# Six places in two hand-written side-work lists: the context's squares and tables, the mixer's mask and turns

## The reference

```python
for l in range(DEPTH):                       # first block, DEPTH = 2
    h  = rmsnorm(x,  norm_g[l]) * (1.0 + scale[:, None]) + shift[:, None]
    hc = rmsnorm(xc, norm_g[l]) * (1.0 + scale_c) + shift_c
    if last:                                 # second layer: context only gives keys and values
        pkv = hc @ w_in[l][:, OFF_K:OFF_POOL]
    q, k, v, up, uf, g = split_proj(h @ w_in[l])
    q = apply_axial_rope(rmsnorm(q, q_norm_g[l]), cos, sin)
    k = apply_axial_rope(rmsnorm(k, k_norm_g[l]), cos, sin)
    ...
# second block ("mixer"): gated spatial part and linear recurrence
h = _rmsnorm(x, norm1_g);  p = h @ w_in      # p = [u, v, g_lru, x_lru]
v = _layernorm(gelu(v)); w = where(tril, ws, 0)
y_gm = gelu(u) * (einsum('hts,bcshd->bcthd', w, v) + bs)
r, i = sigmoid(xr @ wa + ba), sigmoid(xr @ wx + bx)     # xr: causal convolution of x_lru
a = exp(-8 r softplus(-lam));  b = sqrt(-expm1(2 log a)) * (i * xr)
y_lru = scan(a, b) * gelu(g_lru)
x = x + concat(rmsnorm(y_gm), rmsnorm(y_lru)) @ w_out
...                                          # feed-forward part
```

## Time and profile before

| what | value |
|---|---|
| median of 3 runs | 2348.72 us (2347.27 to 2351.4) |
| profiled execution, its own time | 2348.02 us |
| its span, first to last instruction | 2346.2 us |
| mean granted TensorE clock | 0.991 |
| PE busy | 2266.0 us, 97% |
| DVE busy, ACT busy, POOL busy | 1289.2, 1043.3, 269.4 us |
| HBM read | 428.89 MB |

### The profile page before, as it was taken

One profiled execution on the slowest core, in us unless ns is written; L12 is line 12 of the kernel. 1 busy time (PEld: TensorE's weight loads), 2 busy tenths in 40 slices (PEclk: granted clock), 3 DMA queues, 4 the chain that ended last, 5 costly groups with the idle time before them and its releaser, 6 DMA issues.

```text
span 2346.2 us, 30045 instructions
## 1 busy us (share of the span) xinstructions
PE 2266.0 (97%) x11859; PEld 1824.6 (78%) x11859; DVE 1289.2 (55%) x2038; ACT 1043.3 (44%) x1604; POOL 269.4 (11%) x326
## 2 busy tenths in 40 slices
PE   5899999999999989999999998999999999999998
PEld 2477777777777867678888886888888888888887
DVE  3354523332332264555776777677765777567764
ACT  2233333432322255445554565555544555345553
POOL 1010100000010122100020324111100111001111
PEclk8999999999999999999999999999999999999999
DMA  9974433445655375634566544565655655556553
GB/s 352 340 273 147 149 126 117 140 133 168 237 179 177 134 275 193 238 95 160 180 207 205 172 145 153 179 198 180 189 196 189 188 187 182 198 187 188 188 189 116
DMA packets 322427, 437.14 MB, mean 186 GB/s; under 512 B 13848, under 2 KB 220112, under 8 KB 321264
## 3 DMA queue, kind: packets, MB, share of 16 engines
q1 hardware_dynamic: 316800, 413.19, 53.4%
q0 software_dynamic: 3392, 16.90, 1.9%
q10 hardware_dynamic: 2096, 5.15, 0.6%
HBM read 428.89 MB, written 6.29 MB: 185 GB/s over the span
## 4 chain that ended last, share of the span: by engine, by line
PE 86%; DVE 5%; ACT 4%; DMA 2%; issue 2%; POOL 1%; SPq 0%; ACTq 0%; POOLq 0%
PE ps L1333 24%; PE ps L1334 12%; PE ps L1308 8%; PE ps L1310 8%; PE ps L1309 8%; PE ps L1328 5%; PE ps L1330 5%; PE ps L1329 5%; PE ps L1288 3%; ACT SPL L1539 2%; DVE SPL L1782 2%; PE ps L1382 1%; PE ps L1399 1%; DMA RAW<-in_w_in_dram 1%; DMA RAW<-in_ada_w_dram 1%
## 5 line engine op out<-in xcount | busy, mean ns | idle before, releaser
L1782 DVE TENSOR_TENSOR SPL<-RAW,SPL 128x1024 fp32r<-128x1024 f32 x592 | 751.1, 1273 | 598.4 <-ACT SPL L1539 596.0
L1333 PE MATMUL ps<-HS,SPL 128*128 128x512 f32 x2688 | 954.8, 400 | 11.8 <-DVE SPL L1782 9.0
L1539 ACT ACTIVATE SPL<-RAW 128x1024 fp32r<-128x1024 f32 x592 | 622.2, 1055 | 490.3 <-PE ps L1310 171.6
L1334 PE MATMUL ps<-HS,SPL 128*128 128x256 f32 x2688 | 753.8, 280 | 0.0
L1333 PEld LDWEIGHTS ps<-HS,SPL 128*128 128x128 f32 x2688 | 506.2, 188 | 136.6 <-DVE SPL L1782 6.9
L1334 PEld LDWEIGHTS ps<-HS,SPL 128*128 128x128 f32 x2688 | 509.0, 189 | 2.0 <-issue 1.7
L1308 PE MATMUL ps<-SPL,HS 128*128 128x512 f32 x960 | 395.1, 412 | 12.7 <-DVE SPL L1782 5.3
L1310 PE MATMUL ps<-SPL,HS 128*128 128x512 f32 x960 | 376.1, 392 | 0.0
L1309 PE MATMUL ps<-SPL,HS 128*128 128x512 f32 x960 | 375.5, 391 | 0.0
L1308 PEld LDWEIGHTS ps<-SPL,HS 128*128 128x128 f32 x960 | 181.3, 189 | 75.4 <-issue 16.1
L1309 PEld LDWEIGHTS ps<-SPL,HS 128*128 128x128 f32 x960 | 181.4, 189 | 41.4 <-issue 6.3
(11 more groups left out here) (281 smaller groups left out, 1691.8 us busy)
## 6 DMA issues: line engine op xcount, KB each, us to landing
RAW<-in_w_in_dram SPq DMA_DIRECT2D x208, 512.0 KB, 5.8
RAW<-in_ada_w_dram SPq DMA_DIRECT2D x192, 512.0 KB, 4.9
RAW<-in_ffn_w_up_dram SPq DMA_DIRECT2D x192, 512.0 KB, 3.5
RAW<-in_w_out_dram SPq DMA_DIRECT2D x96, 512.0 KB, 4.5
RAW<-in_ffn_w_down_dram SPq DMA_DIRECT2D x96, 512.0 KB, 3.9
x_spill<-XT POOLq DMA_DIRECT2D x2, 2048.0 KB, 14.4
XT<-x_spill POOLq DMA_DIRECT2D x1, 4096.0 KB, 16.5
MM<-in_x_dram ACTq DMA_DIRECT2D x2, 1024.0 KB, 11.4
```

The lines of the kernel that those rows point to most:

```text
L1333: mm(PS[b][:, :], wr, hh, start=k == 0, stop=False, skip_group_check=True)
L1334: m = mm(PS[b][:, 256:512], wl, hh[:, 0:256], start=False, stop=k == KT - 1, skip_group_check=True)
L1539: act(SPL[:, (n - 1) % NSPL, 0, :], raw_of(i), ACT.Copy).then_inc(s_hi, 1)
L1782: tt(w[:, 1, :], raw_of(s["i"]), w[:, 0, :].bitcast(F32), ALU.subtract).then_inc(s_lo, 1)
```

## The change

Both edits are to lists of `hi`. In `begin`, `ends` moves from the third to the second place, `sums` from the fifth to the sixth, `load_tables` from the sixth to the seventh; `rstd` and `tables` keep theirs. In the mixer, `spatial_mask` moves from the ninth place to the sixth, and the two `turn_spatial` from the eleventh and twelfth to the thirteenth and fourteenth; with this, the list is two places longer, and the `keep_x`, `decay` and all that is appended later stand two places later.

```diff
-                hi.extend([idle, idle, ends, idle, sums, load_tables, idle, idle, rstd, idle, tables] + [context_row] * 5)
+                hi.extend([idle, ends, idle, idle, idle, sums, load_tables, idle, rstd, idle, tables] + [context_row] * 5)
...
-        hi.extend([both_a, idle, both_b, lambda: keep_rows((s_bnr, 1), [])] + [idle] * 4 + [lambda: put("spatial_mask"), idle, turn_spatial(0), turn_spatial(1)] + [keep_x(k) for k in range(KT)] + [lambda: put("decay")])
+        hi.extend([both_a, idle, both_b, lambda: keep_rows((s_bnr, 1), [])] + [idle, lambda: put("spatial_mask")] + [idle] * 6 + [turn_spatial(0), turn_spatial(1)] + [keep_x(k) for k in range(KT)] + [lambda: put("decay")])
```

## The result

The changed kernel took 2356.02 us (median of 15 runs, 2350.28 to 2363.71), the kernel before 2351.26 us (15 runs, 2346.95 to 2353.84). The ratio is 1.0025, 95% interval 1.0017 to 1.0033: slower by a quarter per cent. The forecast was 2352.7, on a base of 2348.7. The measured median lies 3.3 us above it, at the very edge of the forecast (2350 to 2356); 2.5 us of this is the base, which had been the median of only three runs. As a shift the forecast was +4.0 us; by the medians it was +4.8 us, by the ratio 5.9 (0.0025 x 2351; interval 4.0 to 7.8).

What follows compares the result with a forecast made beforehand. PE, busy 97% of the span, was taken to bound the kernel, with gaps ahead of matmuls. Terms 0 + (-0.98 + 0.98) + 0.7 + 3.3 = +4.0 us gave median 2352.7; forecast 2350 to 2356, 8-in-10 range 2346 to 2357.5.

Steps and rivals of the forecast that it cites:

- First edit: Context lists in `begin`: the count's 1.87 us wait goes, later waits take the gain back; 0 us, bounds -1.9 to +1.0.
- it lands at about 852 to 853: Third table DMA of the context, started behind ACT's half of chunk 277's split; would make `tables` 0 to 1 us late.
- Mask and turns: Mixer, first turn of the spatial maps: with the mask three chunks ahead, PE's 0.98 us wait for it goes.
- (a): Normalisation of v, chunks 424 and 425: later `decay` makes PE wait, spending the mask's 0.98 us; bounds 0 to +2.5.
- with the same durations: Assumption at v's normalisation: DVE steps take as long as before, so the last `v2` step is ready about 3 us later.
- (b): Convolution and gates, chunks 445 to 448: two gates together ahead of 448, the second waiting; +0.7 us, bounds 0 to +1.
- (c): Exponentials, scans, y, products late in the mixer: first exponential later, last square +3.3 us; bounds 0 to +6.
- Absorbed: Rival: y and product steps have slack, only the wait changes place; 2347.5 to 2350 us, same; chance 0.18.
- faster: Rival: chunk 460 sooner decides, 461 following without a wait, starting before about 1422; -4.2 us, 2344.5; chance 0.13.
- Clock: Rival: longer waits at chunk 424 or 461 bring low-clock spells, up to 2.0 us each; 2354 to 2357; chance 0.11 (or worse).

Runs made afterwards that it cites:

- squares-only run: Kernel before with only the context's squares (`ends`) sooner, count and tables' transfers where they were; stretch near 822 to 942 came out 0.04 us shorter.
- tables-only run: Kernel before with only count and tables' transfers (`sums`, `load_tables`) one list place later, squares unmoved; +3.7 us by the medians.
- mask only: Kernel before with only `spatial_mask` three list places sooner, turns and all behind them where they were; ratio 0.9996.
- The run with this step alone: Kernel before with two empty places ahead of the first `lru_exp`, so only exponentials, scans, y and products come a chunk later; mixer stretch +2.60 us.
- second edit alone: Kernel before with only the mixer's list edit (mask sooner, turns and all behind two places later), `begin` unchanged; mixer stretch +3.48 us.
- shift back at v: Kernel before with the mixer's list edit, two empty places ahead of v's normalisation removed; mixer stretch less a low-clock spell +1.6 us.

## Why the prediction was right, and where it was not

The direction held, and the size to about a microsecond, the second in part by luck. The two traces, less start, spell and pace, give S1 1.77 + S2 4.96 - 1.6 = +5.1 us against the +4.0 of the sum. But four of its terms were off, two by +1.8 and +0.65, two by -0.75 and -0.55, and so more than half of what was too little was made up by what was too much. By its steps:

- **First edit, 0: mis-sized, +1.8.** The count's wait went, and its gain was given back: right, and shown alone by the squares-only run (-0.04). I had it go into the wait at L1374, which did not change; it went at L1360 and L1367. The step that failed is "it lands at about 852 to 853, so `tables` comes 0 to 1 us late". The start was as I had it; but the transfer took 6.1 us (8.0 in the tables-only run) where I used the 5.1 of the earlier trace rows, so `tables` was 1.66 us late. And having written "and with it PE", I still took 0, when that chain had nothing to spare. My own sentence "if `tables` waits for its DMA by more than 1 us, the first edit is" mis-sized came true at 1.25.
- **Mask and turns, -0.98.** Right: the wait went, and where nothing else moves the gain is kept (mask only: -1.1).
- **(a), 0 with the mask's gain counted in: mis-sized, +0.65 (so about 1.6 by itself instead of 0.98).** Chunk 425 starts at 1306.07 against 1300.23: 5.84, less 3.58 at the start of S2 and 1.6 of the spell. The place (chunk 424) was right; the wait was 2.61 us instead of 1 to 2. I weighed the split beside POOL at 2.75 us and said that this spoke for less than a full block. That reading was wrong. In the earlier trace rows POOL ends at 1288.77 + 2.90 = 1291.67 and the split at 1292.74, 1.07 later, though it had started 1.7 us before POOL's end. In the changed kernel POOL ends at 1301.13 and the split, started at 1298.83, at 1302.22: 1.09 later. A free split takes 1.23. In both, the split ended as if DVE had done next to nothing till POOL was through; 2.75 was short only because the split had started later in POOL's time. By the rule of the Trainium skill ("SBUF — State Buffer", section "Who interferes with whom": the later one waits until the other ends) the split would end 1.23 after POOL, and both rows come out to 0.2 us; the trace agrees with the rule. The other wrong step is "with the same durations". L2092 and L2085, ahead of the split of chunk 424, took 0.96 us more beside POOL and the split itself 0.64 more, while the two steps behind it took 0.96 us less than before (1.21 + 1.23 against 1.75 + 1.65). So the split came late, and PE waited there and no longer at `v_mix`.
- **(b), +0.7: wrong, about 0 in sum.** Both pairs of gates now came without a wait (1380.29, 1390.49), -0.7. But the rows of `gm`'s scale at L1360, a chunk later in the list, came 0.7 to 0.8 us late (1344.71), where I had foreseen no wait. Chunk 451 starts 5.79 later against 5.84 at chunk 425.
- **(c), +3.3: right in mechanism, +2.75.** Against chunk 451, the first exponential comes 3.45 us later and so nearer to the output projection (3.1 foreseen), chunk 460 3.4 sooner (3 to 4), chunk 461 waits 2.96, and the last square is 2.8 later (3.3). The run with this step alone gave +2.60 in S2. `y` starts 3.1 us later (1424.97 against 1416.08, less 5.79), so the terms up to there (3.1 - 1.5 + 1.2 = 2.8) were about right; behind it I had -0.5 + 1.0 and the rows show -0.3, so the +1.0 for products and squares was too much.
- **Rivals.** Absorbed and faster are out: chunk 461 started at 1431.19 - 5.79 = 1425.4 in the time of before, past the 1422 from which "faster" would decide. Clock: one spell more than before cost 1.6 us in S2 of the changed kernel's trace, at chunk 402 and not where I looked; whether the change makes spells likelier is not shown (last section).

## What to carry to other kernels

In a hand-written list that is taken by the chunk, the length is an edit by itself: here two empty places cost 4.5 us and the steps that were meant to move were worth 1 us. Count what stands behind an edit in the list until the list runs empty, and look for the engine that has no gap there (DVE, around `decay` and v). A load that is moved later must be priced by the longest landing that such a transfer shows (here 4.9 to 8.0 us for the same one), not by one row; and a chain that another chain waits for gives its lateness on in full.

## What the hardware did that I had not expected

Low-clock spells, mostly of 3 to 4 us, appeared in every trace, and not only behind long waits: ahead of the one at 1227.7 of the kernel before, PE had waited 0.21 us and then run the 16 one-column matmuls of a count (1.92 us, L1455). Windows (us, PE busy with its instructions, granted clock, DMA share, GB/s), changed kernel and kernel before; 1.00 is the upper level, 2.4 GHz:

```profile
1232.00:1242.00 10.00, 7.90 (x32) 0.83 1.02 357
```

```profile
1226.00:1232.00 6.00, 5.50 (x22) 0.72 0.99 276
```

Each holds about 3.4 us at the lower level (10 x 0.17 / 0.5, 6 x 0.28 / 0.5). Before the change they lay ahead of L1481 and only shortened its wait (0.49 instead of 2.10 us); in the changed kernel they lay in chunk 402 and cost 1.6 us (L1481 to the turn: 16.25 us, against 14.64 in the second edit alone). Of the thirteen traces, nine have the spell of this place ahead of L1481, three behind it in chunk 402 (the changed kernel, mask only, shift back at v) and one has none (squares only), though the code around it is the same in all thirteen. What a spell costs depends on whether a wait stands behind it.

PE also has two paces at a granted clock of 1.00. Lines of the same window, 1472 to 1500, with no wait in it; kernel before, then the changed one:

```profile
L1333 PE MATMUL ps<-HS,SPL 128*128 128x512 f32 x80 | 28.3, 399 | 0.0
```

```profile
L1333 PE MATMUL ps<-HS,SPL 128*128 128x512 f32 x82 | 28.5, 394 | 0.0
```

A chunk takes 2.83 us in the one and 2.77 in the other. From the last wait of S2 to the count near 1540 the kernel before took 78.19 us and the changed one 76.72, with the same matmuls. That alone hides 1.5 us of what a single pair of spans is read for; its cause was not looked into.
